# Two decoder blocks on one core: which comes first in a step of the woven stream, the recurrence's stage or the split of a coming weight piece

## The reference, cut to what matters

```python
h = rmsnorm(x, pre_mix_norm[l]) * (1.0 + sc_m) + sh_m
proj = h @ w_in[l]                       # 2048 x 8208
o_hg = hgrn2_group(proj[..., :HG_COLS], lb_all[l], hg_norm[l])
o_gdn = gdn_group(proj[..., HG_COLS:], gdn_conv_w[l], gdn_a_log[l], gdn_dt_bias[l], gdn_norm[l])
y = jnp.concatenate([o_hg, o_gdn], axis=-1) @ w_out[l]
```

## Time and profile before

| | us |
|---|---|
| median of 3 runs | 3092.03 |
| lowest, highest | 3085.4, 3093.89 |
| the profiled execution | 3087.69 |
| its span, first to last instruction | 3085.9 |

### The profile page before, as it was taken

The page is one execution under the profiler, slowest core; times in us unless marked ns, Lnnn a source line. Parts: engine busy times, 40 slices in busy tenths (PEclk is TensorE's granted clock), DMA queues, the critical chain, the costliest instruction groups (busy, mean ns, idle before and its releaser), DMA issues.

```text
span 3085.9 us, 36089 instructions
## 1 busy us (share of the span) xinstructions
PE 2754.6 (89%) x12877; PEld 2293.4 (74%) x12877; DVE 1962.7 (64%) x2076; ACT 1234.2 (40%) x1281; POOL 73.2 (2%) x36
## 2 busy tenths in 40 slices
PE   1498989889699999999969955999989999999997
PEld 1387879677578888888758844788767888888885
DVE  6769688887656666666664442555446666776665
ACT  1244343444344444444434412444334444444443
POOL 0000000211000000000000000000000000000000
PEclk8699999999899999999989965999999999999998
DMA  8796678567376666666636600766545665666663
GB/s 356 233 229 203 170 179 249 176 223 255 106 228 215 205 216 216 213 203 217 197 96 193 181 0 25 220 192 184 172 135 178 190 187 180 190 187 191 187 189 129
DMA packets 268092, 578.30 MB, mean 187 GB/s; under 512 B 19544, under 2 KB 20464, under 8 KB 262256
## 3 DMA queue, kind: packets, MB, share of 16 engines
q1 hardware_dynamic: 268016, 577.27, 61.1%
HBM read 575.11 MB, written 2.10 MB: 187 GB/s over the span
## 4 chain that ended last, share of the span: by engine, by line
PE 68%; issue 16%; DVE 12%; ACT 2%; DMA 2%; SPq 0%; POOL 0%; DVEq 0%; POOLq 0%; ACTq 0%
PE bank L404 21%; PE bank L405 21%; PE bank L409 21%; PE bank L637 4%; DVE acc L1654 3%; PE bank L634 2%; DVE w_lo L394 2%; DVE acc_w L1586 1%; DVE hg_t L1555 1%; DVE gd_t L1845 1%; ACT junk L1112 1%; DVE op_a_lo L1555 1%; DMA raw<-in_w_ff 0%; DVE gd_t L1555 0%; DVE X L1555 0%
## 5 line engine op out<-in xcount | busy, mean ns | idle before, releaser
L394 DVE TENSOR_TENSOR w_lo<-raw,w_hi 128x1024 fp32r<-128x1024 f32 x880 | 1076.4, 1228 | 794.3 <-ACT w_hi L389 793.1
L389 ACT ACTIVATE w_hi<-raw 128x1024 fp32r<-128x1024 f32 x880 | 931.3, 1059 | 1266.2 <-PE bank L409 1119.1
L404 PE MATMUL bank<-w_hi,op_a_hi 128*128 128x512 f32 x2272 | 900.4, 396 | 21.0 <-ACT w_hi L389 12.6
L405 PE MATMUL bank<-w_hi,op_a_lo 128*128 128x512 f32 x2272 | 891.2, 392 | 0.0
L409 PE MATMUL bank<-w_lo,op_a_hi 128*128 128x512 f32 x2272 | 610.8, 391 | 4.7 <-DVE w_lo L394 4.5
L404 PEld LDWEIGHTS bank<-w_hi,op_a_hi 128*128 128x128 f32 x2272 | 430.7, 190 | 110.2 <-issue 22.8
L409 PEld LDWEIGHTS bank<-w_lo,op_a_hi 128*128 128x128 f32 x2272 | 428.1, 189 | 97.4 <-DVE w_lo L394 8.0
L405 PEld LDWEIGHTS bank<-w_hi,op_a_lo 128*128 128x128 f32 x2272 | 430.9, 190 | 88.2 <-issue 1.0
L404 PE MATMUL bank<-w_hi,hid_hi 128*128 128x512 f32 x864 | 341.0, 395 | 8.9 <-DVE hid_lo L1555 6.4
L405 PE MATMUL bank<-w_hi,hid_lo 128*128 128x512 f32 x864 | 337.3, 390 | 0.0
L409 PE MATMUL bank<-w_lo,hid_hi 128*128 128x512 f32 x864 | 231.2, 389 | 0.0
(11 more groups left out here) (223 smaller groups left out, 2039.8 us busy)
## 6 DMA issues: line engine op xcount, KB each, us to landing
raw<-in_w_in SPq DMA_DIRECT2D x264, 512.0 KB, 4.6
raw<-in_w_ff SPq DMA_DIRECT2D x256, 512.0 KB, 3.9
raw<-in_ffn_w_up SPq DMA_DIRECT2D x176, 512.0 KB, 4.5
ada_raw<-in_w_ada SPq DMA_DIRECT2D x96, 512.0 KB, 5.2
raw<-in_ffn_w_down SPq DMA_DIRECT2D x88, 512.0 KB, 4.2
early<-in_w_ada SPq DMA_DIRECT2D x32, 1024.0 KB, 13.2
raw<-in_w_out SPq DMA_DIRECT2D x32, 512.0 KB, 5.0
ada_raw_f<-in_w_ada SPq DMA_DIRECT2D x32, 512.0 KB, 4.7
```

The source lines that it names most:

```text
L389: nc.scalar.activation(w_hi[:, gj % RAW], raw[:, j % RAW], ACT.Copy).then_inc(hi_ready, 1)
L394: nc.vector.tensor_tensor(w_lo[:, gj % RAW], raw[:, j % RAW], w_hi[:, gj % RAW].bitcast(F32), ALU.subtract).then_inc(lo_ready, 1)
L404: nc.tensor.matmul(where[:, t], hi(kt + k, tok), w_hi[:, s, k], start=first and k == 0, stop=False)
L405: nc.tensor.matmul(where[:, t], lo(kt + k, tok), w_hi[:, s, k], start=False, stop=False)
```

## The change

In the loops of ScalarE and VectorE over `n` the split moves from the head of the step to behind the stage. On VectorE the multiply-adds move with it. The loops of TensorE, SyncE and GpSimd stay as they are, and no instruction is added or taken out.

```diff
@@ ScalarE
             for n in range(STEPS):
-                if n + 3 < STEPS:
-                    split_hi(act, 0, n + 3, 0, n + 3)
                 if n % KP == 1 and KP < n <= GEMM["out"] + KP:
                     keep(n // KP - 1)
...
                 next(stage, None)
+                if n + 3 < STEPS:
+                    split_hi(act, 0, n + 3, 0, n + 3)
@@ VectorE
             for n in range(STEPS):
+                c = n - GEMM["out"] - 5
+                if c >= 16 and c % 4 == 0:
+                    add_out(c // 4)
+                next(stage, None)
                 if n + 2 < STEPS:
                     split_lo(dve, 0, n + 2, n + 2)
                 for k in ADA_AT[n]:
                     add_woven_ada(k)
-                c = n - GEMM["out"] - 5
-                if c >= 16 and c % 4 == 0:
-                    add_out(c // 4)
-                next(stage, None)
```

## The result

The changed kernel takes 3106.98 us, the median of five runs (3099.55 to 3108.35), against 3092.03 for the kernel before. The ratio is 1.0048, 95% interval 1.0029 to 1.0066: slower, by 9 to 20 us, which is clear of the noise and small. The forecast was 3092.4, range 3083 to 3102. The profiled execution is the fastest of its five (3099.55, span 3097.8) and stands against 3087.69 for before: 11.9 of the 15 can be looked for in the traces.

What follows compares the result with a forecast made beforehand. TensorE was taken to set the pace of the woven stream, with gaps where VectorE does. Start, gated starts, HGRN starts and group ends summed 0.3 - 2.6 - 2.2 + 4.9 = +0.4, giving 3092.4 us on the median, range 3083 to 3102.

Steps and rivals of the forecast that it cites:

- start: Start of the stream: a tile's wait shrinks by 1.1, but piece 8's load leaves 5.5 later: +0.3, bounds -1.1 and +5.0.
- first gated start: Start of the first gated group: one multiply-add fewer ahead of each stage, so TensorE waits less: -1.3.
- second gated start: Start of the second gated group: one multiply-add fewer ahead of each stage, so TensorE waits less: -1.3.
- turn of the second gated group: End of the second gated group: a multiply-add now stands ahead of the two products TensorE's turn waits for: +1.2.
- sums and first HGRN start: Sums wait for the late last multiply-add, +1.7; then the first HGRN group's query side comes earlier, -1.1.
- end of the first HGRN group: A multiply-add now stands ahead of the two products that TensorE's turn waits for: +1.2.
- second HGRN start: Start of the second HGRN group: a multiply-add ahead of the first query side falls away: -1.1.
- end of the second, and piece 147: End of the second HGRN group: turn delayed, about 0.4 covered by piece 147's existing wait of 0.79 for a load: +0.8.
- The wait of 1.08: Gated group's start, at 259.12: TensorE's wait was forecast to go, with one multiply-add fewer ahead of the stage.
- The turns at the shared read path: HGRN groups: who goes first may change; VectorE first in both, 3088.1, chance 0.13; GpSimd first in both, 3097.8, chance 0.12.
- a level that changed from 5.4 to 6.4: HGRN groups: levels changing from 5.4 to 6.4 us or back would show the forecast wrong.
- Starved loads: Start of the stream: piece 8's late load isn't made good, with TensorE waits at pieces 20 to 34; 3103 or more, chance 0.10.

Runs made afterwards that it cites:

- e5: Changed kernel with the old order on ScalarE and VectorE in steps 0 to 31: 3102.59 us, ratio 1.0043 to the kernel before.
- e6: Changed kernel with SyncE's two loads of gate_rows issued in step 150 instead of 142: 3100.64 us, ratio 1.0032.
- e7: Changed kernel with the second vector's last two multiply-adds moved from steps 31 and 33 of the second gated group to 26 and 29: 3103.75 us.
- e9: Changed kernel with old order in steps 0 to 31, gate_rows loaded in step 150, second vector's last two multiply-adds at steps 26 and 29: 3095.85 us.
- e14: Changed kernel with gate_rows loaded in step 150 and the second vector's last two multiply-adds one step earlier (31 to 30, 33 to 32): 3095.22 us.
- e10: Kernel before with SyncE's two loads of gate_rows issued in step 150 instead of 142: 3089.35 us, ratio 0.9987.
- e3: Changed kernel with VectorE's multiply-adds put back ahead of the stage, so only the splits are moved: 3100.95 us, ratio 1.0027.
- e4: Kernel before with VectorE's multiply-adds behind the stage in every step, splits staying in place: 3096.49 us, ratio 1.0019.
- e13: Kernel before with gate_rows loaded in step 150 and multiply-adds behind the stage only at offsets 6 to 16 of the gated groups: 3088.33 us.
- e2: Kernel before with VectorE's order alone changed, ScalarE keeping its old order: 3107.32 us, ratio 1.0049.
- e1: Kernel before with ScalarE's order alone changed, VectorE keeping its old order: 3123.85 us, ratio 1.0108.

## Why the prediction was wrong, by its steps

The table, after the sum of the prediction. Where several executions have the same order in a stretch, their mean is taken:

| place | forecast | measured | from |
|---|---|---|---|
| start | +0.3 | +1.1 | t31, 4 against 6 executions |
| first gated start | -1.3 | -1.9 | 31-50: 84.1 (six: after, e5, e6, e7, e9, e14) against 86.0 (before, e10) |
| second gated start | -1.3 | -1.0 | 66-90: 115.2 (six) against 116.2 |
| turn of the second gated group | +1.2 | +1.4 | 98-101: 13.8 against 12.4 |
| sums and first HGRN start | +1.7 - 1.1 | +4.7 | 101-112: 62.7 against 58.0 |
| end of the first HGRN group | +1.2 | +1.2 | 112-121 |
| second HGRN start | -1.1 | -0.3 | 121-139: 83.0 (six) against 83.3 |
| end of the second, and piece 147 | +0.8 | +7.3 | 139-146: +1.2; 146-150: 18.1 against 12.0 |

In all +12.5 against the forecast's +0.4 (the two profiled executions lie 11.9 apart, the medians 15.0); the row of the sums and that of piece 147 hold 10.6 of the 12.1 between them.

*Piece 147 is the step that failed.* I had priced the turn's delay and set 0.4 of it against a wait for a load that was there anyway, as if the load left when it did before. I had named the mechanism, "splits, and so the loads they release, come a stage later", and applied it to the start alone; and I had not named its second half, that this load stands in SyncE's queue behind one of `ada_raw`, which hangs on a multiply-add. The load leaves 7.9 before TensorE begins piece 146 in the kernel before, 8.2 with only the splits moved (e3), 6.4 with only the multiply-adds moved (e4), and 4.9 with both. So the multiply-add is what takes the lead first, and the splits add to it only together with it. Here 3.0 of lead are lost, at a place with no stock: 2 MB of `gate_rows` stand right ahead. A wait for a load that already shows, like the 0.79, is a place where any delay of that load counts in full. That moving `gate_rows` takes the whole term away is shown (e6).

*The sums.* The mechanism and the wait were right (1.95 against 1.7; the sum itself slips, since 552.49 + 1.2 is 553.7 and not 553.9, which gives 1.9), the term was not: I took the wait alone. Behind it the clock fell in the sums (5.17 for 3.63), and VectorE, which sets the pace from there, waits for their end, so the delay reached the HGRN group whole, with the turn's 1.2 counted apart. That the place of these two multiply-adds is the cause is shown (e14), and that the clock alone is not.

*The starts* of the groups came out with the sign forecast, the second HGRN start with too little of it. The wait of 1.08 went, and the first query side stands right behind a split (VectorE at 581.13 and 582.26, in the changed kernel):

```profile
581.13 1.22 DVE L394 TENSOR_TENSOR w_lo<-raw,w_hi 128x1024 fp32r<-128x1024 f32 x1
581.25 4.38 POOL L2314 TENSOR_TENSOR hg_t<-hg_t,hg_t 128x512 f32<-128x512 f32 x2 [24.95 <-ACT hg_t L1112]
582.26 2.00 DVE L1555 TENSOR_TENSOR hg_t<-hg_t,hg_t 128x512 f32<-128x512 f32 x1
```

At the second HGRN group the gain did not stay. It came as forecast: the second query side begins 28.2 behind piece 121, against 29.4 before. Then it was lost again at GpSimd's operations. VectorE's third and fourth query side there, before:

```profile
681.07 0.68 DVE L1555 TENSOR_TENSOR hg_t<-hg_t,hg_t 128x512 f32<-128x512 f32 x1
...
686.45 0.69 DVE L1555 TENSOR_TENSOR hg_t<-hg_t,hg_t 128x512 f32<-128x512 f32 x1
```

and in the changed kernel:

```profile
684.97 1.76 DVE L1555 TENSOR_TENSOR hg_t<-hg_t,hg_t 128x512 f32<-128x512 f32 x1
...
691.36 1.77 DVE L1555 TENSOR_TENSOR hg_t<-hg_t,hg_t 128x512 f32<-128x512 f32 x1
```

Between them lie 5.4 before and 6.4 now, and the next level takes 6.5 (5.4 before). Pieces 121 to 127 take 3 to 4 less than before in after, e5 and e6, and 127 to 133 give back 2.2 to 5.0 of it.

At the first gated start the clock has a part: the kernel before has a stretch at half clock from 281.4 to 284.8, the changed one has none and takes 83.8. e9, e14 and e10 each have two such stretches there; e9 and e14 take 85.1 and 85.2, e10 in the old order 86.2. At like clock the gain is 1.0.

*The start of the stream:* the load of piece 8 left at 139.9 as forecast (140); what it cost lay within the bounds, as far as the spread of the executions shows.

*The rivals.* The turns at the shared read path did move in the changed kernel, and the prediction's own sign of being wrong, a level that changed from 5.4 to 6.4, is there in the second HGRN group. In the first query sides it follows the order: in before, e10 and e13 5.6 lie between the first and the second of the second group, and the second takes 0.68 or 0.69. In the nine kernels with the multiply-adds behind the stage there (after, e2, e4 to e9, e14), the distances between the two take 2.4 instead of 1.3, the two lie 6.7 to 6.8 apart, and the second takes 1.75 to 1.77. In the later levels it goes by execution: with no change there, e10's first HGRN group took the short form that the kernel before has in the second, three levels at 5.4 where the kernel before has 6.4:

```profile
604.81 2.91 POOL L2314 TENSOR_TENSOR hg_t<-hg_t,hg_t 128x512 f32<-128x512 f32 x1 [2.46 <-ACT hg_t L1112]
605.86 0.71 DVE L1555 TENSOR_TENSOR hg_t<-hg_t,hg_t 128x512 f32<-128x512 f32 x1
```

So they are in part the order's doing and in part the spread between executions. From the first to the seventh query side the second group takes 33.3 in the three kernels with the old order and 33.5 to 36.7 in the six of the changed one, so this rival holds for part of that group, at up to 3.4, and it leaves most of the loss to the sums and to piece 147. Starved loads happened, not at pieces 20 to 34 as the rival put it but at 147. The range was too narrow because it covered only the places I had listed, and took in neither its own upper bound of the gated starts (0) nor that of the ends (+6); the largest term was one for which I had priced 0.8.

*What stays open.* The kernel with both terms mended (e14) is 4 above the kernel before on the median, with an interval of 1 to 7. Its profiled execution, one of its two fastest, is 1.9 behind at piece 156 (780.5 against 778.6), with 4.7 of loss at the start and gains behind it; since the start wanders by 4 and the part behind piece 156 by 5, no cause can be given for the 4. In e1, whose loss is largest, the medians agree with the stretches; for differences of 4 us one profiled execution, in a kernel whose runs spread over 10, is not enough.

## What to carry to other kernels

When an instruction is moved behind another on one engine, follow what it releases on the in-order queues too: look for each place where a transfer already arrives just in time or late, and count the whole shift there, with everything that stands between it and the queue's head. Ask of a swap on two engines what each half would do alone; the order on one may be what keeps a loop between them open. And before a change is costed to a microsecond, a second profile of the same kernel tells which stretches repeat to 0.1 and which wander by 4, and how far the part wanders that nobody touched.

## What the runs showed of the hardware

TensorE's granted clock fell from 2.4 to 1.2 GHz in or just behind the 32 narrow sums (128 x 1) in nine of the fourteen profiled executions: with a wait of 1.95 ahead of them (they took 5.17), of 0.81 (3.73), and with none (4.47). In the kernel before it did not (3.63), and in e10, with the same order of work, it fell just behind them. Where VectorE set the pace next, a stretch at half clock of 6.8 us (556.8 to 563.6) cost nothing: e7 took 58.8 from 101 to 112 with it, the kernel before 58.7 without one behind its sums.

VectorE's query side with two inputs took 0.71 from 605.86 on, while GpSimd's operation of 2.91 had run since 604.81. The Trainium skill (SBUF — State Buffer, "SBUF: two separate sides") would have it blocked until GpSimd is done. As before the change, this trace has it done inside GpSimd's row, at the cost, if any, of GpSimd's length (2.91 where GpSimd first takes 2.31).
